# Constant products in front of 15 data waits of the tensor engine in a decoder layer

## What is computed

```python
x = x + 0.5 * rmsnorm(swiglu_ffn(rmsnorm(x), ffn1_w_gu, ffn1_w_down))     # width 2816
u = rmsnorm(x) @ w_in                                                      # 4 x 512
c = silu(rmsnorm(causal_dwconv(u_val * sigmoid(u_glu), conv_w) + conv_b))  # 31 taps
a, b = gates(short_conv(u_x)); hs = associative_scan(a, b)                 # RG-LRU
x = x + rmsnorm(concat([c, hs * gelu(u_gelu)]) @ w_out)
x = x + 0.5 * rmsnorm(swiglu_ffn(rmsnorm(x), ffn2_w_gu, ffn2_w_down))
x = x + rmsnorm(sigmoid(rmsnorm(x) @ ple_w_gate) * (p @ ple_w_proj))
```

## Time and profile before

| | us |
|---|---|
| median of 3 runs | 2317.92 |
| lowest, highest | 2313.61, 2321.83 |
| the profiled execution | 2320.19 |
| its span, first to last instruction | 2318.1 |
| PE busy | 2134.7 (92%) |
| DVE busy | 1235.9 (53%) |
| ACT busy | 732.1 (32%) |
| mean granted clock of PE | 0.939 |

### The profile page before, as it was taken

The page is one execution under the profiler, slowest core; times in us unless marked ns, Lnnn a source line. Parts: engine busy times, 40 slices in busy tenths (PEclk is TensorE's granted clock), DMA queues, the critical chain, the costliest instruction groups (busy, mean ns, idle before and its releaser), DMA issues. The chain is left out here.

```text
span 2318.1 us, 34548 instructions
## 1 busy us (share of the span) xinstructions
PE 2134.7 (92%) x13032; PEld 2116.8 (91%) x13032; DVE 1235.9 (53%) x2468; ACT 732.1 (32%) x1436; POOL 44.3 (2%) x80
## 2 busy tenths in 40 slices
PE   5899999999999878999888889999999999985886
PEld 5899999999999778999888789999999999985885
DVE  4444445444555676454556654554543454557676
ACT  4411212221122243344565422121221121225563
POOL 0000000000000011230000000000000000000000
PEclk8999999999999989976899899999999999998897
DMA  4071111101111011222023201111100111102222
GB/s 151 31 107 46 54 54 55 45 18 45 54 54 54 1 41 31 71 37 46 19 74 109 91 1 55 55 54 54 54 35 28 45 54 54 54 1 74 74 91 75
DMA packets 160509, 124.55 MB, mean 54 GB/s; under 512 B 72744, under 2 KB 151916, under 8 KB 160432
## 3 DMA queue, kind: packets, MB, share of 16 engines
q1 hardware_dynamic: 124272, 113.95, 15.7%
q10 hardware_dynamic: 34112, 8.52, 2.2%
q0 software_dynamic: 2048, 1.06, 0.3%
HBM read 114.35 MB, written 9.15 MB: 53 GB/s over the span
## 5 line engine op out<-in xcount | busy, mean ns | idle before, releaser
L669 PE MATMUL ps<-x_hi,w_lo 128*128 128x352 f32 x2688 | 886.6, 330 | 18.7 <-DVE w_lo L1587 9.7
L670 PE MATMUL ps<-x_lo,w_hi 128*128 128x352 f32 x2688 | 876.1, 326 | 0.0
L671 PE MATMUL ps<-x_hi,w_hi 128*128 128x352 f32 x2688 | 874.9, 325 | 0.0
L669 PEld LDWEIGHTS ps<-x_hi,w_lo 128*128 128x128 f32 x2688 | 518.1, 193 | 20.0 <-DVE w_lo L1587 10.4
L670 PEld LDWEIGHTS ps<-x_lo,w_hi 128*128 128x128 f32 x2688 | 518.1, 193 | 0.0
L671 PEld LDWEIGHTS ps<-x_hi,w_hi 128*128 128x128 f32 x2688 | 516.2, 192 | 0.0
L669 PE MATMUL ps<-a_hi,wd_lo 128*128 128x352 f32 x1104 | 361.5, 327 | 26.2 <-DVE a_lo L1684 11.6
L670 PE MATMUL ps<-a_lo,wd_hi 128*128 128x352 f32 x1104 | 357.8, 324 | 0.0
L671 PE MATMUL ps<-a_hi,wd_hi 128*128 128x352 f32 x1104 | 357.8, 324 | 0.0
L1734 DVE TENSOR_TENSOR acc<-ps,acc 128x352 f32<-128x352 f32 x480 | 249.2, 522 | 90.9 <-PE ps L671 84.2
L1667 DVE TENSOR_TENSOR tmp_u<-ps,rstd_pre 128x352 f32<-128x352 f32 x132 | 69.0, 523 | 363.0 <-PE ps L671 363.0
(11 more groups left out here) (207 smaller groups left out, 1690.0 us busy)
## 6 DMA issues: line engine op xcount, KB each, us to landing
raw<-in_ffn_w_gu_dram SPq DMA_DIRECT2D x88, 512.0 KB, 3.6
rawd<-in_ffn_w_down_dram SPq DMA_DIRECT2D x22, 1024.0 KB, 7.1
raw<-in_w_out_dram SPq DMA_DIRECT2D x24, 512.0 KB, 3.5
raw<-in_ple_w_gate_dram SPq DMA_DIRECT2D x24, 512.0 KB, 3.4
raw<-in_w_in_dram SPq DMA_DIRECT2D x16, 512.0 KB, 3.8
toeplitz<-rev ACTq DMA_DIRECT2D x8, 512.0 KB, 8.3
x_in<-in_x_prompt_dram ACTq DMA_DIRECT2D x6, 512.0 KB, 7.9
out_dram<-y_stage SPq DMA_DIRECT2D x6, 512.0 KB, 2.6
```

Of the source, the lines that this page charges most:

```text
L669: eng.matmul(dst, wl, xh, start=first, stop=False)
L670: eng.matmul(dst, wh, xl, start=False, stop=False)
L671: return eng.matmul(dst, wh, xh, start=False, stop=last)
```

## The change

The tile `ones` becomes an F32R tile, and its old users read it as float32. `keep_busy(n, dst)` issues n products of that tile with itself, 128 x 128 weights on 128 columns, into a bank that is free; nothing reads them, and the next real product there starts afresh. `busy_before` first waits for the auxiliary bank, which `norm_sum` did behind its other wait. The products stand before the wait for the data:

- in front of `norm_sum`: `pre2` chunk 0 and `pre4` chunk 0 (60 each), `pre2` chunk 1 (150), `conv` chunk 0 (50), `pre3` chunks 0, 1, 2 (100, 150, 110), `post4` chunks 1, 2 (40, 80);
- in `p_to_features` before the transposes of chunk 2 (90), and in `ple_unit(0, 1)` before a spread and the sum of `post3` chunk 2 (30);
- before the spread of `conv` chunk 1 (60), before the third chunk's input projection (60), and before the first gate products at the start (40);
- before the down products of chunks 0 and 1 in the last step of both layers, and of chunk 2 in the first step of the second (18 each, five times).

That is 19 places in the stream and 1170 products. Everything else stays.

```diff
--- before.py
+++ after.py
@@ -223,7 +223,8 @@
         std = tile("std", [P, 8])
         sq, sq_at, _ = place("sq", [P, SQ, C])
         ident = tile("ident", [P, P])
-        ones = tile("ones", [P, P])
+        ones_r = tile("ones", [P, P], F32R)
+        ones = ones_r.bitcast(F32)
         params = tile("params", [P, 3 * P])
         half_g = tile("half_g", [P, 2 * KT])
         eps_t = tile("eps_t", [P, 1])
@@ -670,6 +671,18 @@
                 eng.matmul(dst, wh, xl, start=False, stop=False)
                 return eng.matmul(dst, wh, xh, start=False, stop=last)
 
+            def keep_busy(n, dst):
+
+
+                for _ in range(n):
+                    eng.matmul(dst[:, 0:P], ones_r[:, :], ones_r[:, :], start=True, stop=True)
+
+            def busy_before(name, c, n):
+
+                at = AUX["norm", NORM[name, c]]
+                eng.wait_ge(aux_free, at - 1)
+                keep_busy(n, ps_aux[:, at % 2, :])
+
             def wide(s, k, t):
                 sl = slice(k * WIDE + t * P, k * WIDE + t * P + P)
                 return w_hi[s][:, sl], w_lo[s][:, sl]
@@ -722,8 +735,11 @@
                                     start=True, stop=True)
                 mm.then_inc(aux_full, 1)
 
-            def down_products(f, i, c):
+            def down_products(f, i, c, busy=0):
                 Q, off = NI * NC * G * f, down_at(f, i, c)
+                if busy:
+                    bank_at(i * STEP, off)
+                    keep_busy(busy, ps[:, off % BANKS, :])
                 eng.wait_ge(a_lo_done, i * (NC * G) + (Q + 2 * c + 2))
                 for m in range(KT):
                     bank_at(i * STEP, off + m)
@@ -770,10 +786,11 @@
                     if c == 1:
                         down_ready(f, 0)
                         down_products(f, 0, 0)
+                        busy_before("pre3", 2, 110)
                         norm_sum("pre3", 2)
                         down_products(f, 0, 1)
                         norm_spread("pre3", 2)
-                down_products(f, 0, 2)
+                down_products(f, 0, 2, 18)
 
             def ffn_last(f, post, pre):
 
@@ -788,6 +805,7 @@
                                 norm_spread(post, 0)
                         if c == 2:
                             if t == 1:
+                                busy_before(pre, 0, 60)
                                 norm_sum(pre, 0)
                             if t == 2:
                                 norm_spread(pre, 0)
@@ -797,12 +815,13 @@
                     gate_products(f, i, c, hook)
                     if c == 0:
                         down_ready(f, i)
-                    down_products(f, i, c)
-
-            def norms_behind(post, pre):
+                    down_products(f, i, c, 18 if c < 2 else 0)
+
+            def norms_behind(post, pre, busy):
 
                 def hook(n):
                     if n == 1:
+                        busy_before(pre, 1, busy)
                         norm_sum(pre, 1)
                     if n == 2:
                         norm_spread(pre, 1)
@@ -836,6 +855,7 @@
                         mm = eng.transpose(dst[:, 2 * P + 32 * j:2 * P + 32 * j + 32],
                                            st_rows[0:32, j * P:j * P + P], ident[0:32, 0:32])
                     mm.then_inc(psum_full, 1)
+                    keep_busy(40, bank(gate_at(0, 0, 0)))
                     eng.wait_ge(wide_lo, 2)
                 start_products(gate_at(0, 0, c), SPECS[:2], c)
                 norm_sum("pre1", c)
@@ -853,8 +873,10 @@
 
 
             eng.wait_ge(wide_lo, 2 * (WIDE0["mix"] + 1))
-            behind = norms_behind("post1", "pre2")
+            behind = norms_behind("post1", "pre2", 150)
             for c in range(NC):
+                if c == 2:
+                    keep_busy(60, bank(RING["vg", 2, 0]))
                 eng.wait_ge(x_lo_done, PAIRS * (c + 1))
                 for n in range(4):
                     if (c, n) == (0, 2):
@@ -921,8 +943,12 @@
 
             def gelu_hook(n):
                 if n % 4 == 3:
+                    if n == 3:
+                        busy_before("conv", 0, 50)
                     norm_sum("conv", n // 4)
                 if n % 4 == 0 and n:
+                    if n == 8:
+                        keep_busy(60, bank(RING["in", 7, 1, 1]))
                     norm_spread("conv", n // 4 - 1)
 
             in_unit(6, gelu_hook)
@@ -958,6 +984,7 @@
                         norm_spread("conv", 2)
                     return
                 if c > 1 and n == 1:
+                    busy_before("pre3", c - 2, (100, 150)[c - 2])
                     norm_sum("pre3", c - 2)
                 if n == 2:
                     if c > 1:
@@ -984,10 +1011,12 @@
             def p_to_features():
                 eng.wait_ge(p_read, 16 * 10)
                 for c in range(NC):
+                    if c == 2:
+                        busy_before("pre4", 1, 90)
                     for k in range(PT):
                         to_features(lambda i: p_in[:, i, :], RING["pT", c, k], c, k)
 
-            behind = norms_behind("post3", "pre4")
+            behind = norms_behind("post3", "pre4", 0)
 
             def ple_unit(c, q):
                 v = WIDE0["ple"] + 4 * c + q
@@ -997,6 +1026,8 @@
                 for t in range(2):
                     tile_product(bank(RING["ple", c, q, t]), v % 2, t, c)
                     if (c, t) == (0, 0) and q in (1, 2):
+                        if q == 1:
+                            keep_busy(30, bank(RING["ple", 0, 1, 1]))
                         behind(1 + q)
                 if (c, q) == (0, 0):
                     p_to_features()
@@ -1039,11 +1070,13 @@
             ple_unit(2, 0)
             norm_spread("post4", 0)
             ple_unit(2, 1)
+            busy_before("post4", 1, 40)
             norm_sum("post4", 1)
             ple_unit(2, 2)
             to_tokens(0)
             norm_spread("post4", 1)
             ple_unit(2, 3)
+            busy_before("post4", 2, 80)
             norm_sum("post4", 2)
             norm_spread("post4", 2)
             to_tokens(1)
```

## The result

| | before | after |
|---|---|---|
| median of 11 runs | 2317.92 | 2331.45 |
| lowest, highest | 2311.95, 2324.98 | 2323.11, 2336.01 |
| the profiled execution | 2320.19 | 2330.95 |
| its span | 2318.1 | 2329.1 |
| mean granted clock | 0.939 | 0.958 |

The ratio is 1.0057, with a 95% interval of 1.0044 to 1.0070: the change costs 13.5 us. The forecast was +8; the median lies in the range 2298 to 2334 and in the forecast's own range, 2318 to 2334.

The account below looks back on a forecast made before the run. PE, busy for 92% of the span, was taken to set the pace, through its waits and clock. Terms -10.1 + 1.1 + 5.9 + 11.1 = +8.0 us gave 2326 us from the median 2317.9; range 2298 to 2334, the forecast's own 2318 to 2334.

Parts of the forecast that it names:

- Rival 1: Added products cost only 0.06 us (0.107 at low clock), so every fill ends inside its wait: -18, 2300 us; chance 0.20.
- rival 2: The fill raises the clock also from the low level, after 5.5 us: sum -4.6, 2313 us; chance 0.15.
- rival 3: The fill doesn't hold the clock even from 2.4 GHz: sum over +100, beyond 2420 us; chance 0.07.
- C, +5.9: At `pre2` chunk 1, `pre3` chunks 1 and 2, `post4` chunk 2 the fill outlasts the wait: +5.9 us.
- the terms +1.7, +2.1, +1.2 and +0.9: Predicted delays in us at `pre2` chunk 1, `pre3` chunk 1, `pre3` chunk 2 and `post4` chunk 2, in that order.
- D, +11.1: Fills beginning at the low clock: start +2.1 and the 90 products before the side input's chunk 2 transposes +9.0 us.
- nothing covers it: The 90-product fill's lateness passes in full to the transposes, `p` and gate products behind it: +9.0 us.
- A, -10.1: Places where the fill is shorter than the wait or nearly so and PE is last afterwards: -10.1 us.
- B, +1.1: `pre2`, `pre4`, `pre3` chunk 0 and `conv` chunk 1 spread: the reciprocal, not PE's clock, sets the end; +1.1 us.
- +1.5 for one or two new falls of the clock: New 2 to 3 us waits for the reciprocal behind the `pre2`, `pre4`, `pre3`, `conv` fills: clock falls cost +1.5 us.
- 0.45: Share of a low-clock stretch's length given back at high clock, with PE full and nothing else ending later.
- -0.4 of gain: Total saving booked for `pre2`, `pre4`, `pre3` chunk 0 and the `conv` chunk 1 spread together: -0.4 us.

Follow-up runs that it names:

- width runs: The changed kernel, same places and counts, with every added product 256 or 32 columns wide instead of 128: 2321.13 and 2400.06 us.
- four unchanged profiles: The kernel before (2317.92 us) and three runs of the change with every count at zero, F32R `ones` and moved waits kept: 2318.71, 2317.25, 2314.74 us.
- B: The change with only `pre2`, `pre4`, `pre3` chunk 0 and the `conv` chunk 1 spread filled, 280 products: 2326.45 us, ratio 1.0036 to before.
- C: The change with only `pre2` chunk 1, `pre3` chunks 1 and 2 and `post4` chunk 2 filled, 490 products: 2324.24 us, ratio 1.0025 to before.
- A: The change with only the 18-product places, mixer, `conv` chunk 0 sum, gate and `post4` chunk 1 filled, 270 products: 2318.14 us, ratio 0.9992 to before.
- run 4: Kernel B plus 20 or 22 products before the spreads of `pre2`, `pre4`, `pre3` chunk 0 and `conv` chunk 2: 2323.11 us, ratio 1.0017 to before.
- D: The change with only the start (40) and the side input's chunk 2 transposes (90) filled, 130 products: 2328.58 us, ratio 1.0041 to before.
- the two fitted kernels: 256-column products, counts fitted to waits where PE comes last: 2308.37 us, ratio 0.9942 to before; then without four late places: 2310.33 us, ratio 0.9956.

## Why the prediction was right and where it was wrong

**The price.** 0.111 and 0.213 were read from the distance of weight loads beside wide products, and the streams show 0.111 to 0.112 and 0.213 to 0.215. Rival 1 (0.06) is out, and the width runs show why: the load, not the columns, is the price. It could have had a smaller chance than 0.20, since the trace before has streams of narrow instructions, of plain float32, in the convolution, the first pair at clock 1.0 and the second at 0.5:

```profile
986.47 3.69 PE L900 MATMUL ps_aux<-gt_even,toep_first 128*128 128x48 f32 x32
989.98 4.16 PE L900 MATMUL ps_aux<-gt_even,toep_mid 128*128 128x48 f32 x32
...
1083.53 7.02 PE L900 MATMUL ps_aux<-gt_last,toep_mid 128*128 128x48 f32 x32
1090.33 0.64 PE L669 MATMUL ps_aux<-xc_hi,gw_lo 128*128 128x352 f32 x1
```

32 instructions of 48 columns take 3.51 us, 0.110 each, and 6.80 us, 0.213 each; columns alone would make them 0.02 and 0.04, by the same 0.159 and 0.291 for 352. The Trainium skill (TensorE: Matmul & The Clock Gate, section LDWEIGHTS) puts a load at the number of its columns over 1.2, 107 ns here; the trace agrees at the high clock, while at the low clock it shows 0.213, which the rule doesn't have. The 81 ns that the same page of the Trainium skill (section Back-to-back issue gap) gives for a stream of 128 columns was not met by these F32R products, at 111; the section doesn't name the type that it was measured in.

**The clock.** That 128 columns hold the high clock and don't raise the low one was right at all 19 places: the clock stays low in the two fills that begin low and high in the other 17, with 1.00 over 26.6 us from 845.37 and 0.50 over 27.4 us from 2134.71. The ground for it was weak, though: of the 82 instructions in the stretch at 1078.44 58 are 48 columns wide and 24 are 352 wide, none like the added ones. Rivals 2 and 3 are out for 128 columns. What rival 2 says came with 256 columns, and what rival 3 says with 32, whose +81 is near the 100 that it was given.

**C, +5.9**, came to +5.4. PE ends late by what the fill is longer than the wait; the terms +1.7, +2.1, +1.2 and +0.9 measured +1.4, +1.9, +0.8 and +1.3.

**D, +11.1**, came to +9.0. The start was +1.8 for +2.1. The side input was +7.2 for +9.0: the transposes do stand 13.6 later, of which 4.9 is the shift with which the stage begins, so 8.7 late as forecast. The step that made it too dear is "nothing covers it". Behind the transposes and the sum PE waited 1.51 in the trace before:

```profile
2141.49 1.33 PE L708 MATMUL ps_aux<-ones,ssum 128*128 128x1 f32 x6
2144.33 0.63 PE L669 MATMUL ps<-a_hi,wd_lo 128*128 128x352 f32 x1 [1.51 <-issue]
```

and after there is no such wait. It took up 1.5 of the delay.

**A, -10.1**, came to -7.0. The mixer (-2.3 for -2.0) and the `conv` sum (-1.0 for -1.0) were right. The 18-product places gave -1.8 for -3.0 against the mean of the four: I booked the two low stretches of before's profile as if every execution had them, and of the four unchanged profiles one has none at 761 and two have none at 2041. The same holds for `post4` 1 (-0.9 for -1.5), where the unchanged stages spread over 1.5 us, B and C without a fill there have 23.80 and 23.79, and A with it 24.84, so no gain of that fill is shown. The gate gave -1.0 for -2.6, the largest miss in A: 30 products stand before the spread, one operation ahead of the sum that waits, and 1.40 of that wait stays idle; the clock still falls behind it, for 3.4 us.

**B, +1.1**, came to +3.8, alone to +6.6 in its stages. The term that was too small is "+1.5 for one or two new falls of the clock". The new waits of 2 to 3 us were foreseen, with their places at 817 and 2096 (816.92, and 2102.17 where the work stands 4.9 later); so was that the clock may fall there. The size was off: it fell in both, for 6.8 and 3.4 us, and 0.45 of that is 3.1 and 1.5 in front of products that nothing covers. That the -0.4 of gain was next to nothing is shown by run 4.

**The convolution stretch, no term**, came to +4.7. The forecast put it at nothing without saying so, and it is most of the 5.4 that the forecast lacked. The added products end before it and its operations are the same. What it loses is clock. By each trace's record of the granted clock, PE has the low clock in it for 92.2 us in all four unchanged profiles and in D, for 99.0 in B, C, the 32 wide and the two fitted kernels, and for 102.4 in the change, A, the 256 wide and run 4. At the forecast's own 0.45 the 6.8 and 10.2 us more are +3.1 and +4.6; measured are +3.3 to +3.9 and +4.7 to +5.8. Only D's +1.1 isn't in that.

What carries the effect from the added products to the clock there is open. The runs speak against chance alone (four unchanged profiles alike), against the count (60 ahead of it in B, 96 in A, 150 in C: +3.3, +5.3, +3.9) and against the time from the start of the span at which it begins: after enters it at 965.07 and takes 168.60, an unchanged stream enters at 965.01 and takes 163.65. That time isn't yet the place of the clock's falls: the first one comes 7.6 to 7.8 us behind the entry in the four unchanged profiles, and 5.7 in after and 5.2 in A. But it comes at 7.6 in B and 7.8 in run 4 too, which are long, so it doesn't decide alone.

The forecast's sum was 8.0 and the runs give 13.4: A 3.1 too good, B 2.7 too low, C and D 2.6 too high, the convolution 4.7 missing, and the rest of the program 2.6 shorter. So the price of a product, the clock in the fills, C and the places in B were right for the reasons given. That the sum came as near as 5 us owes something to luck: A, B and the convolution came out 10.5 above it, C, D and the rest 5.2 below.

## What to carry to other kernels

In this kernel constant products that keep the tensor engine's clock up paid only in waits behind which that engine comes last, and only up to the length of the wait: nine places and 349 products give 8 us, thirteen and 543 give 12, and nineteen with 1170 cost 13.5. Count a fill by its weight load (here 0.111 us at 2.4 GHz, 0.213 at 1.2), try it wider as long as the spacing doesn't grow (256 columns here), don't let it begin behind an unfilled wait, and ask what the engine will wait for next when it comes earlier. Look too at stretches that the change doesn't touch: one here had 7 to 10 us more of low clock in nine of ten changed kernels. Judge by stage durations over several profiles of the unchanged kernel: busy share and granted clock both improved in the kernel that got slower.

## What the runs showed that I had not expected

- A product with 128 x 128 F32R weights costs 0.111 us at 32, 128 and 256 columns; the kernels with 256 and 32 columns, with the same counts at the same places, lie 79 us apart (2321.13 and 2400.06), and their fills differ in the clock and not in the price.
- The fill of 150 products at 32 columns shows PE busy for 27.47 of 27.47 us at a granted clock of 0.59; a full row of busy time doesn't tell that the clock is high.
- The convolution stretch takes 163.7 to 164.2 in all four profiles of the unchanged stream and 167.2 to 169.7 in all but one of the changed ones. The low clock in it is 92.2 us in the first and 99.0 or 102.4 in the second; why it is longer stays open.
- Which short waits put the clock down differs between executions of one kernel: the stretch at 2041 is there in two of four. The Trainium skill (TensorE: Matmul & The Clock Gate, section What's actually happening) says that one kernel shows different numbers of slow products at its start from run to run. The traces here show the same later in the kernel, with the low stretch of 3.4 us at 2041 in two of four. A saving of such a stretch should be booked at its share of executions.
